# Forget logits of a gated attention layer computed beside the first head's projection instead of by matmuls of their own

## The chip, the cores and the metric

The kernel runs on one core of a Trainium2 chip. A core has a matmul engine (TensorE, "PE" in the profile, with its weight loads shown apart as "PEld"), a vector engine (DVE), a scalar engine (ACT), GpSimd (POOL), and queues that start DMAs (here almost all from SyncE, SP). The engines run side by side, each through its own list of instructions in order, and wait for each other through semaphores. The metric is the device time of one execution in microseconds (us). Positions in the trace are given in us from the start of the span.

## What is computed

Two residual layers over x of 512 tokens by 1024. Layer 0 is block attention with rotary; layer 1 is forgetting attention, cut here to what matters:

```python
hdn = rms_norm(x, norm_g[i])                       # (1, 512, 1024)
proj = hdn @ b_w_in[j]                             # 4 * 1024 + 8 columns
q, k, v, z = jnp.split(proj[..., :4 * WIDTH], 4, axis=-1)
f_logit = (proj[..., 4 * WIDTH:] + b_f_bias[j]).astype(jnp.float32)
log_f = jax.nn.log_sigmoid(f_logit).transpose(0, 2, 1)   # (1, 8 heads, 512)
c = jnp.cumsum(log_f, axis=-1)
sc = q @ k.T * scale + (c[..., :, None] - c[..., None, :])
x = x + (merge_heads(softmax(mask(sc)) @ v) * jax.nn.silu(z)) @ w_out[i]
```

So each of the 8 heads needs one forget logit for each token: 8 columns of the input projection beside the 4096 of q, k, v and z. Their log sigmoids are summed along the tokens.

## The kernel before

Everything stays in SBUF. Each fp32 operand of a matmul is held as two fp32r tensors, a rounded high part and the rest (`_hi`, `_lo`), and each product is made of three matmuls (`three`, L321: high by high, high by low, low by high). The profile gives these three lines as L325, L326 and L327.

A "job" is one set of weights of 1024 by 512: a head's q, k, v and z columns, or half of an output projection. It comes in 8 chunks (k = 0 to 7) of 128 rows. For each chunk SP starts a DMA into `w_raw` (a ring of 4), ACT rounds it into `w_hi` (L586), and POOL writes the rest into `w_lo` (L1061). There are two slots of `w_hi` and `w_lo`, so that the next head's weights are made ready while PE works with this head's. PE waits for the last low part (`wlo_set`) before it starts the projection of a head.

For each head PE projects q, k and v of the four token tiles t (`qkv`, L372: 24 matmuls of 384 columns each, with the hidden state as stationary operand), and z of all tokens at once (`zproj`, L392: 24 matmuls of 512 columns). After each tile ACT sums the squares of q and k and copies v (`read_qkv`), POOL makes the root (`rstd_qk`: an add, L1077, and a power, L1079), and DVE writes v's low part (L801) and the normed q and k (L811). `turn_qk` transposes them on PE (L408), ACT and DVE split the result (`split_qk`, L631 and L835), and `scores` makes the products. In layer 1 `scores` also adds the summed logs by a matmul with `crows` (L429), for which PE waits on `c_set`. `period` interleaves a head's attention with the projection of the next head, so that PE has matmuls while other engines do the softmax. The order on each engine is written out by hand in `first`, `period` and `last`; nothing else sets it.

The forget logits are made once, in `first(1)`, between the tiles 1 and 2 of the second layer's first head. `forget` (L476) runs 16 matmuls of 512 columns with `wf` as stationary operand, a tensor of 40 columns whose first 8 hold the high part of the 8 weight columns and whose last 8 the low part. The result is 40 rows by 512 tokens in bank 4. ACT copies the low rows (L697), DVE adds the two and the bias (L933) and makes the negative absolute value (L936), ACT runs Exp (L701) and Ln (L703), DVE makes the log sigmoid (L942) and its running sum (`cumulate`, a scan over 512 tokens on 8 partitions, L946). ACT rounds the sums into `crows` (L709), DVE writes their rest (`split_c`, L951) and sets `c_set`.

ACT loads a table of functions (ACT_TABLE_LOAD) before Ln and again before the next Exp.

## Time and profile before

| what | value |
|---|---|
| median of 3 runs | 568.36 us (568.06 to 568.9) |
| the profiled execution: its own time | 567.49 us |
| its span | 565.7 us, 9786 instructions |
| granted TensorE clock | 1.0 of full speed |
| PE busy | 558.7 us of the span, 3118 matmuls |
| DVE, ACT, POOL busy | 342.6, 249.7, 268.2 us |

The span is what lies between the first and the last instruction; the execution's own time is 1.79 us longer. Busy time of PE is modelled, since matmuls overlap: the distance from one matmul's start to the next one's tells what one costs in a row of them.

### The profile page before, as it was taken

What the parts mean: (1) busy time and instruction counts of PE and PEld (TensorE: products, weight loads), DVE (VectorE), ACT (ScalarE), POOL (GpSimd) and SP (SyncE); (2) the same over time, 40 slices, a digit from 0 to 9 for tenths busy, and PEclk for the clock granted to TensorE, in tenths of its full rate; (3) what the DMA queues carried; (4) which work ended last, traced back from release to release, by engine and by line L of the source; (5) the groups of instructions that cost most, each with busy time, mean ns of one, the idle gap of its engine ahead of it and who ended that gap; (6) DMA issues with size and microseconds to landing.
All of it is one profiled execution on the core that took longest, in us unless ns stands there. A gap on an engine that the chain in (4) does not pass through costs nothing.

```text
span 565.7 us, 9786 instructions
## 1 busy us (share of the span) xinstructions
PE 558.7 (99%) x3118; PEld 516.2 (91%) x3118; DVE 342.6 (61%) x824; ACT 249.7 (44%) x762; POOL 268.2 (47%) x320
## 2 busy tenths in 40 slices
PE   6999999999999999999999999999999999999998
PEld 4999999999999999888888999999999999998887
DVE  3788585859594949473553755656565646464621
ACT  5737272626263636152544635444444444442400
POOL 5857272727171818162656454545353536360700
PEclk9999999999999999999999999999999999999999
DMA  9823132313131313123423261415140615030221
GB/s 263 231 61 110 57 93 57 94 56 93 56 93 56 96 52 104 45 76 110 123 68 83 83 102 34 104 35 130 28 121 24 112 30 130 24 124 2 74 94 56
DMA packets 77068, 47.82 MB, mean 85 GB/s; under 512 B 3953, under 2 KB 71281, under 8 KB 77042
## 3 DMA queue, kind: packets, MB, share of 16 engines
q1 hardware_dynamic: 77040, 47.49, 31.5%
q8 instruction: 14, 0.23, 0.2%
q14 instruction: 12, 0.10, 0.1%
q10 hardware_dynamic: 2, 0.00, 0.0%
HBM read 45.39 MB, written 2.10 MB: 84 GB/s over the span
## 4 chain that ended last, share of the span: by engine, by line
PE 98%; DMA 1%; SPq 0%; DVE 0%; ACT 0%; issue 0%
PE banks L325 26%; PE banks L326 26%; PE banks L327 26%; PE banks L456 5%; PE banks L441 3%; PE banks L408 2%; PE banks L426 2%; PE banks L430 2%; PE banks L425 2%; PE banks L357 1%; DMA first_raw<-in_a_w_in_dram 1%; PE banks L429 1%; PE banks L482 0%; PE banks L483 0%; SPq L292 0%; DVE hT_lo L782 0%
## 5 line engine op out<-in xcount | busy, mean ns | idle before, releaser
L1061 POOL TENSOR_TENSOR w_lo<-w_raw,w_hi 128x512 fp32r<-128x512 f32 x147 | 188.3, 1311 | 63.0 <-ACT w_hi L586 63.0
L325 PE MATMUL banks<-w_hi,hT_hi 128*128 128x384 f32 x512 | 175.6, 343 | 1.0 <-DVE hT_lo L782 1.0
L327 PE MATMUL banks<-w_hi,hT_lo 128*128 128x384 f32 x512 | 171.6, 335 | 0.0
L326 PE MATMUL banks<-w_lo,hT_hi 128*128 128x384 f32 x512 | 171.6, 335 | 0.0
L1077 POOL TENSOR_TENSOR msq<-ssq,eps 128x2 f32<-128x2 f32 x64 | 14.3, 224 | 186.4 <-ACT junk L622 186.3
L325 PEld LDWEIGHTS banks<-w_hi,hT_hi 128*128 128x128 f32 x512 | 96.5, 188 | 1.9 <-POOL w_lo L1061 1.6
L326 PEld LDWEIGHTS banks<-w_lo,hT_hi 128*128 128x128 f32 x512 | 96.5, 189 | 0.1
L327 PEld LDWEIGHTS banks<-w_hi,hT_lo 128*128 128x128 f32 x512 | 96.3, 188 | 0.0
L586 ACT ACTIVATE w_hi<-w_raw 128x512 fp32r<-128x512 f32 x148 | 85.0, 646 | 20.2 <-DMA w_raw<-in_b_w_in_dram 14.4
L622 ACT ACTIVATE junk<-banks 128x128 bf16<-128x128 f32 x128 | 34.3, 274 | 115.8 <-PE banks L327 115.8
L906 DVE RECIPROCAL gz<-gz 128x128 f32<-128x128 f32 x64 | 58.1, 931 | 0.5
L835 DVE TENSOR_TENSOR qkT_lo<-banks,qkT_hi 128x512 fp32r<-128x512 f32 x32 | 20.6, 686 | 56.2 <-ACT qkT_hi L631 56.2
L801 DVE TENSOR_TENSOR v_lo<-banks,v_hi 128x128 fp32r<-128x128 f32 x64 | 18.2, 286 | 57.0 <-ACT v_hi L625 56.8
L325 PE MATMUL banks<-w_hi,yT_hi 128*128 128x512 f32 (+1 forms) x136 | 51.9, 382 | 0.0
L327 PE MATMUL banks<-w_hi,yT_lo 128*128 128x512 f32 (+1 forms) x136 | 51.3, 377 | 0.0
L326 PE MATMUL banks<-w_lo,yT_hi 128*128 128x512 f32 (+1 forms) x136 | 51.2, 377 | 0.0
L326 PE MATMUL banks<-hT_lo,w_hi 128*128 128x512 f32 x128 | 50.0, 391 | 0.0
L325 PE MATMUL banks<-hT_hi,w_hi 128*128 128x512 f32 x128 | 49.9, 390 | 0.0
L327 PE MATMUL banks<-hT_hi,w_lo 128*128 128x512 f32 x128 | 49.9, 390 | 0.0
L1079 POOL TENSOR_TENSOR rstd<-msq,power 128x2 f32<-128x2 f32 x64 | 44.3, 692 | 5.0
L641 ACT ACTIVATE probs<-banks,negmax 128x512 f32<-128x512 f32 (+1 forms) x64 | 33.3, 526 | 29.3 <-DVE negmax L856 28.9
L631 ACT ACTIVATE qkT_hi<-banks 128x512 fp32r<-128x512 f32 x32 | 17.4, 596 | 62.5 <-PE banks L408 62.5
(113 smaller groups left out, 883.9 us busy)
## 6 DMA issues: line engine op xcount, KB each, us to landing
w_raw<-in_b_w_in_dram SPq DMA_DIRECT2D x64, 256.0 KB, 3.7
w_raw<-in_a_w_in_dram SPq DMA_DIRECT2D x52, 256.0 KB, 3.0
w_raw<-in_w_out_dram SPq DMA_DIRECT2D x32, 256.0 KB, 2.9
first_raw<-in_a_w_in_dram SPq DMA_DIRECT2D x12, 256.0 KB, 5.6
out_dram<-xs SPq DMA_DIRECT2D x7, 256.0 KB, 2.1
xs<-in_x_dram SPq DMA_DIRECT2D x3, 512.0 KB, 5.8
xs<-in_x_dram SPq DMA_DIRECT2D x2, 256.0 KB, 3.2
gz<-in_norm_g_dram SPq DMA_DIRECT2D x1, 512.0 KB, 3.7
```

What stands on the lines that cost most here:

```text
L325: pe.matmul(dst, ah, bh, start=first and m == 0, stop=False)
L326: pe.matmul(dst, ah, bl, start=False, stop=False)
L327: mm = pe.matmul(dst, al, bh, start=False, stop=last and m == n - 1)
L456: mm = pe.matmul(banks[:, Y_BANK, j * P:SEQ], a[:, s, j, :], b[:, PT_COL[j]:PT_COL[j] + w], start=n == 0, stop=n == len(work) - 1)
L586: act.activation(w_hi[:, slot, k, :], raw, ACT.Copy).then_inc(whi_set, 1)
L622: sq = act.activation(junk[:, m, :], banks[:, qkv_bank(layer, h, t), m * P:(m + 1) * P], ACT.Square, scale=SCALE, accum_out=ssq[:, t % 2, ...
L641: act.activation(probs[:, P_COL[t]:P_COL[t] + w], banks[:, bank, col:col + w], ACT.Exp, bias=negmax[:, t:t + 1], accum_out=rowsum[:, t:t + ...
L801: dve.tensor_tensor(v_lo[:, s, t, :], banks[:, qkv_bank(layer, h, t), 2 * P:3 * P], f32(v_hi[:, s, t, :]), ALU.subtract).then_inc(vlo_set, 1)
L835: dve.tensor_tensor(qkT_lo[:, m, :], banks[:, QT_BANK + m, :], f32(qkT_hi[:, m, :]), ALU.subtract).then_inc(qkTlo_set, 1)
L906: dve.reciprocal(part, part).then_inc(ez1_set, 1)
L1061: pool.tensor_tensor(w_lo[:, slot, k, :], raw, f32(w_hi[:, slot, k, :]), ALU.subtract).then_inc(wlo_set, by)
L1079: pool.tensor_tensor(rstd[:, t % 2, :], msq[:, t % 2, :], power[:, :], ALU.pow).then_inc(rstd_set, 1)
```

## The change

Rows of `w_hi` and `w_lo` grow from 512 to 528 columns. The job's weights sit at columns 16 to 527, and columns 8 to 15 of slot 0 hold the 8 forget columns, written once in layer 0 from `wf_raw` by ACT and DVE. Nothing else is written there, so that they are still in place when slot 0 holds the second layer's first head. For this head alone the projection's matmuls take columns 8 to 399: 392 instead of 384. Each of the four tiles then has its 8 logits ahead of q, k and v in the same bank, and all reads of the bank are shifted by 8 columns (`qkv_cols`).

`forget` and its 16 matmuls are gone. DVE adds the bias to each tile's 128 by 8 logits (`read_forget`), and all four tiles' logits (128 by 32) go through the log sigmoid in one go in `rot`. PE turns the four 128 by 8 pieces into 8 rows by 512 tokens in bank 4 (`turn_forget`, between `zproj` and `turn_qk`), and the scan reads them from there. On ACT, Exp and Ln now stand behind the reading of tile 3 and ahead of the rounding of the last two weight chunks of the next head, and `exp_z` ahead of `crows`. The bias comes by a broadcasting DMA of 128 by 8, issued by SP between the layers ahead of the second layer's weights; the small DMA at the start and POOL's zeroing of `wf` (L1087) are gone.

```diff
+W_AT = 16
+F_AT = W_AT - HEADS
+WIDE = W_AT + CH
...
-        w_hi = sb("w_hi", [P, 2, KC, CH], F32R)
-        w_lo = sb("w_lo", [P, 2, KC, CH], F32R)
+        w_hi = sb("w_hi", [P, 2, KC, WIDE], F32R)
+        w_lo = sb("w_lo", [P, 2, KC, WIDE], F32R)
...
-        wf = sb("wf", [P, KC, LO_ROW + HEADS], F32R)
-        fbias = sb("fbias", [HEADS, 1])
...
+        def q_at(layer, h):
+            return HEADS if layer == 1 and isinstance(h, int) and h == 0 else 0
+        def qkv_cols(layer, h, t, first, n=1):
+            at = q_at(layer, h) + first * P
+            return banks[:, qkv_bank(layer, h, t), at:at + n * P]
...
-        f_lo, f_all = spare[0:HEADS, 0:SEQ], spare[0:HEADS, SEQ:2 * SEQ]
-        f_exp = rot[:, :, :, :].rearrange("p a b n -> p (a b n)")[0:HEADS, :]
+        f_all = spare[0:HEADS, SEQ:2 * SEQ]
+        f_log = rot[:, 0, 0, :].rearrange("p (f t h) -> p f t h", f=4, t=TILES)
         ones = cos_t[:, :, :, :].rearrange("p a b n -> p (a b n)")[0:HEADS, SEQ:2 * SEQ]
+        fbias = cos_t[:, 1, 0, 0:HEADS]
...
-                sp.dma_start(fbias[:, :], b_f_bias[0].rearrange("(h o) -> h o", o=1)).then_inc(small_in, 16)
...
+                    sp.dma_start(fbias, b_f_bias[0].partition_broadcast(P)).then_inc(qk_gain_in, 16)
...
-                    mm = three(banks[:, qkv_bank(layer, h, t), 0:3 * P],
+                    cols = slice(W_AT - q_at(layer, h), W_AT + 3 * P)
+                    mm = three(banks[:, qkv_bank(layer, h, t), 0:cols.stop - cols.start],
                                [((hT_hi[:, k, t * P:(t + 1) * P], hT_lo[:, k, t * P:(t + 1) * P]),
-                                 (w_hi[:, slot, k, 0:3 * P], w_lo[:, slot, k, 0:3 * P]))], k == 0, k == KC - 1)
+                                 (w_hi[:, slot, k, cols], w_lo[:, slot, k, cols]))], k == 0, k == KC - 1)
...
+                if q_at(layer, h):
+                    pe.wait_ge(wf_split, 2)
+                    wait(pe, f_step, t - 1)
...
-            def forget():
-                pe.wait_ge(wf_split, 2)
-                pe.wait_ge(hTlo_set, 2 * TILES * LAYERS)
-                pe.wait_ge(pTlo_set, 3 * HEADS)
-                for k in range(KC):
-                    pe.matmul(banks[0:LO_ROW + HEADS, FORGET_BANK, :], wf[:, k, :], hT_hi[:, k, :], start=k == 0, stop=False)
-                    mm = pe.matmul(banks[0:LO_ROW + HEADS, FORGET_BANK, :], wf[:, k, :], hT_lo[:, k, :],
-                                   start=False, stop=k == KC - 1)
+            def turn_forget():
+                pe.wait_ge(f_step, 7)
+                for t in range(TILES):
+                    mm = pe.transpose(banks[0:HEADS, FORGET_BANK, t * P:(t + 1) * P], f_log[:, 3, t, :], ident[:, :])
                 mm.then_inc(f_done, 1)
...
-                    qkv(layer, 0, 0, 1)
-                    forget()
-                    qkv(layer, 0, 0, 2)
-                    qkv(layer, 0, 0, 3)
+                    for t in range(1, TILES):
+                        qkv(layer, 0, 0, t)
                 zproj(layer, 0, 0)
+                if layer == 1:
+                    turn_forget()
                 turn_qk(layer, 0)
...
-                    act.wait_ge(small_in, 32)
-                    act.activation(wf[:, :, 0:HEADS], wf_raw[:, :, :], ACT.Copy).then_inc(wf_split, 1)
+                    act.wait_ge(small_in, 16)
+                    act.activation(w_hi[:, 0, :, F_AT:W_AT], wf_raw[:, :, :], ACT.Copy).then_inc(wf_split, 1)
...
-                    act.wait_ge(f_done, 1)
-                    act.activation(f_lo, banks[LO_ROW:LO_ROW + HEADS, FORGET_BANK, :], ACT.Copy).then_inc(f_act, 1)
                     read_qkv(layer, 0, 0, 2)
                     split_w(layer, 1, 1, (4, 5))
-                    act.wait_ge(f_step, 2)
-                    act.activation(f_exp, f_exp, ACT.Exp, scale=-1.0).then_inc(f_act, 1)
-                    act.wait_ge(f_act, 2)
-                    act.activation(f_exp, f_exp, ACT.Ln, bias=1.0).then_inc(f_act, 1)
                     read_qkv(layer, 0, 0, 3)
+                if layer == 1:
+                    act.wait_ge(f_step, 5)
+                    act.activation(f_log[:, 1], f_log[:, 1], ACT.Exp, scale=-1.0).then_inc(f_act, 1)
+                    act.wait_ge(f_step, 6)
+                    act.activation(f_log[:, 2], f_log[:, 1], ACT.Ln).then_inc(f_act, 1)
                 split_w(layer, 1, 1, (6, 7))
+                exp_z(layer, 0)
                 if layer == 1:
-                    act.wait_ge(f_step, 4)
+                    act.wait_ge(f_step, 8)
                     act.wait_ge(consts_set, 1)
                     act.activation(crows[0:HEADS, :], f_all, ACT.Copy).then_inc(chi_set, 1)
-                exp_z(layer, 0)
                 split_qk(layer, 0)
...
-            def forget_logits():
+            def read_forget(t):
+                dve.wait_ge(vhi_set, TILES * HEADS + t + 1)
+                dve.tensor_tensor(f_log[:, 0, t, :], banks[:, t % 2, 0:HEADS], fbias[:, :], ALU.add).then_inc(f_step, 1)
+            def log_sigmoid():
+                f, e, ln, lf = (f_log[:, n] for n in range(4))
+                dve.wait_ge(f_step, TILES)
+                dve.scalar_tensor_tensor(out=e, in0=f, scalar=-1.0, in1=f, op0=ALU.mult,
+                                         op1=ALU.max).then_inc(f_step, 1)
                 dve.wait_ge(f_act, 1)
-                dve.scalar_tensor_tensor(out=f_all, in0=banks[0:HEADS, FORGET_BANK, :], scalar=fbias[:, 0:1], in1=f_lo,
-                                         op0=ALU.add, op1=ALU.add).then_inc(f_step, 1)
-                dve.wait_ge(f_step, 1)
-                dve.scalar_tensor_tensor(out=f_exp, in0=f_all, scalar=-1.0, in1=f_all, op0=ALU.mult,
-                                         op1=ALU.max).then_inc(f_step, 1)
+                dve.tensor_scalar(e, e, 1.0, None, ALU.add).then_inc(f_step, 1)
+            def log_forget():
+                f, e, ln, lf = (f_log[:, n] for n in range(4))
+                dve.wait_ge(f_act, 2)
+                dve.scalar_tensor_tensor(out=lf, in0=f, scalar=0.0, in1=ln, op0=ALU.min,
+                                         op1=ALU.subtract).then_inc(f_step, 1)
             def cumulate():
-                dve.wait_ge(f_act, 3)
-                dve.scalar_tensor_tensor(out=f_lo, in0=f_all, scalar=0.0, in1=f_exp, op0=ALU.min,
-                                         op1=ALU.subtract).then_inc(f_step, 1)
-                dve.wait_ge(f_step, 3)
+                dve.wait_ge(f_done, 1)
                 dve.wait_ge(ones_set, 1)
-                dve.tensor_tensor_scan(f_all, ones, f_lo, 0.0, ALU.mult, ALU.subtract).then_inc(f_step, 1)
+                dve.tensor_tensor_scan(f_all, ones, banks[0:HEADS, FORGET_BANK, :], 0.0, ALU.mult,
+                                       ALU.subtract).then_inc(f_step, 1)
...
-                    dve.tensor_tensor(wf[:, :, LO_ROW:LO_ROW + HEADS], wf_raw[:, :, :], f32(wf[:, :, 0:HEADS]),
+                    dve.tensor_tensor(w_lo[:, 0, :, F_AT:W_AT], wf_raw[:, :, :], f32(w_hi[:, 0, :, F_AT:W_AT]),
                                       ALU.subtract).then_inc(wf_split, 1)
                 else:
-                    dve.wait_ge(qk_gain_in, 32)
+                    dve.wait_ge(qk_gain_in, 48)
                     dve.tensor_scalar(cos_t[:, 0, 0, :], cos_t[:, 0, 0, :], SCALE, None, ALU.mult).then_inc(tables_set, 1)
                     dve.wait_ge(tables_set, 3)
+                    read_forget(0)
                     split_v(layer, 0, 0, 0)
                     split_hidden(layer, TILES - 1)
                     norm_qk(layer, 0, 0)
-                    split_v(layer, 0, 0, 1)
-                    norm_qk(layer, 0, 1)
-                    forget_logits()
-                    split_v(layer, 0, 0, 2)
-                    norm_qk(layer, 0, 2)
-                    split_v(layer, 0, 0, 3)
-                    norm_qk(layer, 0, 3)
+                    for t in range(1, TILES):
+                        read_forget(t)
+                        if t == TILES - 1:
+                            log_sigmoid()
+                        split_v(layer, 0, 0, t)
+                        norm_qk(layer, 0, t)
+                    log_forget()
                     cumulate()
...
-            pool.memset(f32(wf[:, :, :]), 0.0)
...
```

PE, from the end of z's projection of the second layer's first head to the next head's first matmuls. In the other operands `ident` is the unit matrix and `rot` holds the logs. Before:

```order
L326 MATMUL banks<-hT_lo,w_hi 128x512
L327 MATMUL banks<-hT_hi,w_lo 128x512
L408 MATMUL banks<-ident,qkn 128x128 [waits y_gated,qkTlo_set,qkn_set]
L408 MATMUL banks<-ident,qkn 128x128 x7
L325 MATMUL banks<-w_hi,hT_hi 128x384 [waits wlo_set,qkn_set]
```

With the change:

```order
L338 MATMUL banks<-hT_lo,w_hi 128x512
L339 MATMUL banks<-hT_hi,w_lo 128x512
L497 MATMUL banks<-ident,rot 8x128 [waits f_step]
L497 MATMUL banks<-ident,rot 8x128 x3
L424 MATMUL banks<-ident,qkn 128x128 [waits y_gated,qkTlo_set,qkn_set]
L424 MATMUL banks<-ident,qkn 128x128 x7
L337 MATMUL banks<-w_hi,hT_hi 128x384 [waits wlo_set,qkn_set]
```

Four transposes, behind a wait for the logs (`f_step`), have come in ahead of the eight of q and k; the wait for the next head's low weight parts (`wlo_set`) follows them as before.

ACT, from the Exp of the logs to the split of the turned q and k, with the reading of tile 3 (`junk`, `v_hi`) in it. Before:

```order
L701 ACTIVATE rot<-rot 8x512 [waits f_step]
L703 ACT_TABLE_LOAD
L703 ACTIVATE rot<-rot 8x512 [waits f_act]
L622 ACTIVATE junk,ssq<-banks 128x128 [waits ssq_set,rstd_set,a_done]
L622 ACTIVATE junk,ssq<-banks 128x128
L625 ACTIVATE v_hi<-banks 128x128
L586 ACTIVATE w_hi<-w_raw 128x512 [waits raw_in2]
L586 ACTIVATE w_hi<-w_raw 128x512 [waits raw_in3]
L709 ACTIVATE crows<-sin_t 8x512 [waits consts_set,f_step]
L662 ACT_TABLE_LOAD [waits gate_set]
L662 ACTIVATE gz<-banks 128x512 [waits z_done]
```

With the change:

```order
L635 ACTIVATE junk,ssq<-banks 128x128 [waits ssq_set,rstd_set,a_done]
L635 ACTIVATE junk,ssq<-banks 128x128
L638 ACTIVATE v_hi<-banks 128x128
L714 ACTIVATE rot<-rot 128x32 [waits f_step]
L716 ACT_TABLE_LOAD
L716 ACTIVATE rot<-rot 128x32 [waits f_step]
L599 ACTIVATE w_hi<-w_raw 128x512 [waits raw_in2]
L599 ACTIVATE w_hi<-w_raw 128x512 [waits raw_in3]
L675 ACT_TABLE_LOAD [waits gate_set]
L675 ACTIVATE gz<-banks 128x512 [waits z_done]
L722 ACTIVATE crows<-sin_t 8x512 [waits consts_set,f_step]
```

The Exp, the table load and the Ln have moved from ahead of the reading of tile 3 to between it and the last two weight roundings, and the rounding of the sums (`crows`) has moved behind z's Exp.

DVE, from the normed q and k of tile 2 to the scan. Before:

```order
L801 TENSOR_TENSOR v_lo<-banks,v_hi 128x128 [waits vhi_set]
L811 SCALAR_TENSOR_TENSOR qkn<-banks,rstd,cos_t 128x128 [waits qkn_set,rstd_set]
L811 SCALAR_TENSOR_TENSOR qkn<-banks,rstd,cos_t 128x128
L942 SCALAR_TENSOR_TENSOR sin_t<-sin_t,rot 8x512 [waits f_act]
L946 SCALAR_TENSOR_TENSOR sin_t<-cos_t,sin_t 8x512 [waits ones_set,f_step]
```

With the change:

```order
L945 TENSOR_TENSOR rot<-banks,cos_t 128x8 [waits vhi_set]
L951 SCALAR_TENSOR_TENSOR rot<-rot 128x32 [waits f_step]
L954 TENSOR_SCALAR rot<-rot 128x32 [waits f_act]
L813 TENSOR_TENSOR v_lo<-banks,v_hi 128x128 [waits vhi_set]
L823 SCALAR_TENSOR_TENSOR qkn<-banks,rstd,cos_t 128x128 [waits qkn_set,rstd_set]
L823 SCALAR_TENSOR_TENSOR qkn<-banks,rstd,cos_t 128x128
L960 SCALAR_TENSOR_TENSOR rot<-rot 128x32 [waits f_act]
L967 SCALAR_TENSOR_TENSOR sin_t<-cos_t,banks 8x512 [waits ones_set,f_done]
```

Three small steps have come in ahead of tile 3's v and q, k, one of them behind a wait for ACT's Exp; the scan's second input is now the bank (`banks`), and it waits for PE's transposes (`f_done`).

## Rows read from the trace of the kernel before

**Rows 1.** The page: busy time by engine, and the chain that ended last.
```profile
PE 558.7 (99%) x3118; PEld 516.2 (91%) x3118; DVE 342.6 (61%) x824; ACT 249.7 (44%) x762; POOL 268.2 (47%) x320
...
PE 98%; DMA 1%; SPq 0%; DVE 0%; ACT 0%; issue 0%
```
**Rows 2.** Timeline of PE (start, us, what): first forget matmul, first of tile 2.
```profile
294.96 0.40 PE L482 MATMUL banks<-hT_hi,wf 128*40 128x512 f32 x1
...
298.68 0.33 PE L325 MATMUL banks<-w_hi,hT_hi 128*128 128x384 f32 x1
```
**Rows 3.** Timeline of PE, from tile 3's last matmul to the first scores.
```profile
306.84 0.33 PE L327 MATMUL banks<-w_hi,hT_lo 128*128 128x384 f32 x1
307.02 0.39 PE L325 MATMUL banks<-hT_hi,w_hi 128*128 128x512 f32 x1
...
312.50 1.04 PE L408 MATMUL banks<-ident,qkn 128*128 128x128 f32 x8
313.30 0.42 PE L325 MATMUL banks<-w_hi,hT_hi 128*128 128x384 f32 x1
...
317.54 0.39 PE L425 MATMUL banks<-qkT_hi 128*128 128x512 f32 x1
```
**Rows 4.** Timeline of ACT, from the table load to the rounding of the sums.
```profile
305.40 1.28 ACT L703 ACT_TABLE_LOAD   x1
306.70 0.63 ACT L703 ACTIVATE rot<-rot 8x512 f32<-8x512 f32 x1
307.24 0.26 ACT L622 ACTIVATE junk<-banks 128x128 bf16<-128x128 f32 x1
...
307.74 0.27 ACT L625 ACTIVATE v_hi<-banks 128x128 fp32r<-128x128 f32 x1
307.89 1.16 ACT L586 ACTIVATE w_hi<-w_raw 128x512 fp32r<-128x512 f32 x2
312.94 0.63 ACT L709 ACTIVATE crows<-sin_t 8x512 fp32r<-8x512 f32 x1 [3.89 <-DVE sin_t L946]
```
**Rows 5.** Groups by line and shape: busy us, mean ns of one.
```profile
L689 ACT ACTIVATE wf<-wf_raw 128x64 fp32r<-128x64 f32 x1 | 0.3, 258 | 0.0
...
L982 DVE TENSOR_TENSOR wf<-wf_raw,wf 128x64 fp32r<-128x64 f32 x1 | 0.2, 214 | 0.0
```
**Rows 6.** Timeline of POOL beside it: tile 3's root, the last two low parts.
```profile
307.92 0.20 POOL L1077 TENSOR_TENSOR msq<-ssq,eps 128x2 f32<-128x2 f32 x1 [0.69 <-ACT junk L622]
308.19 0.69 POOL L1079 TENSOR_TENSOR rstd<-msq,power 128x2 f32<-128x2 f32 x1
308.85 1.29 POOL L1061 TENSOR_TENSOR w_lo<-w_raw,w_hi 128x512 fp32r<-128x512 f32 x1
...
310.09 1.74 POOL L1061 TENSOR_TENSOR w_lo<-w_raw,w_hi 128x512 fp32r<-128x512 f32 x1
```
**Rows 7.** Timeline of DVE beside it, from the log sigmoid to q and k.
```profile
309.45 1.23 DVE L942 SCALAR_TENSOR_TENSOR sin_t<-sin_t,rot 8x512 f32<-8x512 f32 x1
310.71 2.19 DVE L946 TENSOR_TENSOR_SCAN sin_t<-cos_t,sin_t 8x512 f32<-8x512 f32 x1
...
313.61 0.68 DVE L951 TENSOR_TENSOR crows<-sin_t,crows 8x512 fp32r<-8x512 f32 x1 [0.52 <-ACT crows L709]
316.00 1.29 DVE L835 TENSOR_TENSOR qkT_lo<-banks,qkT_hi 128x512 fp32r<-128x512 f32 x2 [1.72 <-ACT qkT_hi L631]
```
**Rows 8.** Timeline of SP, POOL and PE where the second layer begins.
```profile
258.00 0.43 SPq L311 DMA_DIRECT2D cos_t<-in_b_q_norm_dram  x1
258.48 0.43 SPq L312 DMA_DIRECT2D cos_t<-in_b_k_norm_dram  x1
...
281.72 3.02 POOL L1061 TENSOR_TENSOR w_lo<-w_raw,w_hi 128x512 fp32r<-128x512 f32 x2 [0.67 <-ACT w_hi L586]
...
285.32 0.42 PE L325 MATMUL banks<-w_hi,hT_hi 128*128 128x384 f32 x1
```

29 lines of the change are left out of this document (15 added, 14 removed).

## The prediction, made before the changed kernel was run

> **What bounds the kernel.** I read the page first. PE is busy in 99% of the span and makes 98% of the chain that ended last [rows 1], so the time is the sum of what PE issues plus the few moments in which it waits. A microsecond taken from PE's list counts in full, if nothing that PE waits for comes due in its place. What other engines gain or lose counts only there. Next comes PE's timeline at the place of the change, for the distance from one start to the next [rows 2, 3]. Last come the timelines of ACT, POOL and DVE beside it, for how much earlier than PE they finish [rows 4, 6, 7].
>
> **What PE loses.** The 16 forget matmuls start at 294.96 and the first matmul of tile 2 follows at 298.68 [rows 2]: 3.72 us, nothing hidden.
>
> **What PE gets: wider projections.** 96 matmuls take 8 more columns. From 298.68 to 307.02 lie 48 matmuls of 384 columns [rows 2, 3], 0.1738 us each; from 307.02 to 312.50 lie 24 of 512 [rows 3], 0.2283 each. The difference is 0.0546 us for 128 columns, so 8 columns cost 0.0034 and 96 such matmuls 0.33 us. No row shows a width of 392 or a weight row of 528 columns. From below the eight columns cost 0 (a price by blocks of columns), from above what a 512-column matmul costs, 96 x 0.0546 = 5.2 us. I take 0.33, since the two widths shown lie on one line with a small constant (0.1738 - 384 x 0.00043 = 0.01 us).
>
> **What PE gets: four transposes.** Eight transposes take 313.30 - 312.50 = 0.80 us [rows 3], 0.10 each. The new ones move 128 columns too, with 8 columns of weights instead of 128. From above 0.40 us, from below what 128 columns alone cost at the rate above, 4 x 0.055 = 0.22. I take 0.40, the same operation at the same place.
>
> **The sum without waits** is -3.72 + 0.33 + 0.40 = -2.99 us.
>
> **New waits.** I count from P, the end of the first head's q, k, v projection (307.02 in rows 3). With the change PE reaches the end of z's projection at P+5.48 as before, ends the four transposes at P+5.88 and the eight at P+6.68, and then needs the next head's last low weight part; the scores come 4.24 us later (317.54 - 313.30), at P+10.92. Three things must be there.
>
> (a) The logs, for the four transposes, at P+5.48. Tile 3's last matmul ends at 307.17, ACT's reading starts at P+0.22, and v_hi ends at 308.01, P+0.99 [rows 3, 4]. DVE adds the bias (about 0.2, as the 64-element step took 0.214 [rows 5]) and starts on the negative absolute value at P+1.22, ending about P+1.4. ACT's Exp takes about 0.25 (64 elements took 0.258 [rows 5]), to P+1.7. The table load takes 1.28 and Ln follows it at once (305.40 + 1.28 = 306.68, Ln at 306.70 [rows 4]); DVE's addition of one hides behind the load. Ln ends at about P+3.2 and the log sigmoid at P+3.5: 2 us early, no cost.
>
> (b) The low weight parts of the next head, at P+6.68. This chain got longer, since Exp, load and Ln now stand ahead of the last two roundings. ACT starts on chunk 6 at about P+3.1 and ends it at P+3.75 (two take 1.16 [rows 4]); POOL's two parts take 1.29 and about 1.25 [rows 6], to P+6.35. Before it was 311.83, P+4.81, against a need at P+6.28: 1.47 us of slack fall to 0.3. Even that rests on DVE's step at P+1.22 starting freely. POOL's power for tile 3 ran from 308.19 for 0.69, P+1.17 to P+1.86 [rows 6]. Now look at the other pair: DVE's log sigmoid with both inputs in SBUF began at 309.45, while POOL worked until 310.14, and took 1.23, and the same size with POOL idle took 0.68 [rows 6, 7]. It ran, then, from 310.00 to 310.68, and POOL's next part took 1.74 instead of 1.29. One waits for the other to end. If the power holds DVE's step (both inputs in SBUF) likewise, the whole chain moves by about 0.55 us, to P+6.9, and PE waits 0.2 us and then loads its first weights without cover, 0.1 more: 0.3 us. If DVE's step comes first, 0. I take 0.3, as the power's start is 0.05 us ahead by these rows. The Trainium skill ("SBUF — State Buffer", "SBUF: two separate sides") calls this an exclusive lock, held for a whole instruction, when DVE has two SBUF inputs; by that rule the step waits too, and the trace agrees with the rule in the pair above.
>
> (c) The sums (`c_set`) and the turned q and k, at P+10.92. From the end of z's projection, Z = P+5.48: the transposes end at Z+0.64 (eight took 1.04, the next start was 0.24 before that), DVE scans from Z+0.69. If the scan takes 2.19 as before, `crows` runs from Z+2.92 to Z+3.55, its rest to Z+4.27, and q and k (1.29 [rows 7], the first overlapping) to Z+5.48, P+10.96: 0.04 us late, with PE's weights uncovered 0.1 to 0.2 us. But the old scan began at 310.71, while POOL's part ran until 311.83, and both its inputs were in SBUF; by the reading above its own work was about 1.1 us. The new one reads the bank, so I take 1.1 and no cost, with 1.0 us of slack. This end too reaches from 0 to 0.2.
>
> **What is hidden.** DVE's four small additions lie where DVE is idle; they delay v and q, k of their tile by 0.2 us, and PE needs these two tiles later. The bias DMA makes SP's queue about 0.47 us longer (258.00 to 258.48 for the like [rows 8]) ahead of the second layer's weights. PE needs their last low part at 285.32; it was done at 284.74 [rows 8], and that was set by ACT's order behind PE's transposes, not by the load. Cost 0; uncovered it would be 0.47. POOL's zeroing and the early DMA lie beside PE's start, which waits for the input: 0.
>
> **The sum.** -2.99 + 0.3 = -2.7 us against the execution's own 567.49: 564.8. The median of the runs is 0.87 higher, so I forecast 568.36 - 2.7 = 565.7.
>
> **Rivals.**
> - The low weight parts come much later: ACT's chain is on PE's path, and every us in it costs one. Were a switch of tables to cost a second load time (another 1.28), they would be ready at P+7.6 to 8.2, PE would wait 1.0 to 1.6, and the time would be 566.4 to 567.0. Against it: Ln followed the load by 0.02 us [rows 4]. The Trainium skill ("ScalarE: Activation LUTs", "What ACT_TABLE_LOAD costs") gives a switch 2.66 us with a drain, which is this rival; the row speaks against it.
> - No new wait at all, and transposes near their lower end: -3.72 + 0.33 + 0.22 = -3.17, 565.2.
> - Slower than before: a 392-column matmul is billed as a 512-column one, at 96 places, because it is no whole number of 128-column pieces or crosses the pieces of a row. Price 5.2 instead of 0.33: +2.2 us, 570.6. It decides from 0.03 us extra a matmul on. Nothing in the trace has such a width, so I can't exclude it; that q, k and v are one piece of 384 in the same bank speaks against it.
> - The change takes PE's work away and the time is given back, since a transfer or another engine sets the pace of the second layer: 567.4 to 568.9. Against it: PE is idle in 1% of the span, and other engines are at most 61% busy [rows 1].
>
> **How the numbers follow.** Forecast, with 0 to 0.5 us of waits (565.3 to 566.0): 0.62. No wait and cheap transposes (565.0 to 565.3): 0.15. Late weights (566.0 to 567.2): 0.14. Given back: 0.05. Slower: 0.04. The range leaves out the last two and little more of the others: 564.9 to 566.9. A measurement of this kernel can tell about 0.2%, 1.1 us. Faster by more than that (below 567.2): 0.91; within: 0.05; slower: 0.04.
>
> **What would show it.** In the profile of the changed kernel: no 40-column matmuls; 392-column matmuls 0.177 us apart; four transposes in 0.2 to 0.4 us; the log chain with its load between tile 3's v and chunk 6; the low part of chunk 7 ending within 0.4 us of PE's need; a scan of about 1.1 us. Wrong would be a wait of PE over 0.5 us at the next head's first projection or at its scores, or another distance of the wide matmuls.

## The result: slower, by 3.9 us

| | median of the runs, us | lowest to highest | profiled execution | its span |
|---|---|---|---|---|
| before | 568.63 (4 runs) | 568.06 to 569.48 | 567.49 | 565.7 |
| changed | 572.52 (4 runs) | 571.67 to 572.62 | 571.67 | 569.9 |

The ratio is 1.0067, with a 95% interval of 1.0051 to 1.0083. The forecast was 565.7, faster. The time lies 6.8 us above it and outside the range.

The page of the changed kernel, busy time by engine and the chain that ended last, answers to [rows 1]:

```profile
PE 562.6 (99%) x3106; PEld 518.9 (91%) x3106; DVE 340.7 (60%) x828; ACT 248.2 (44%) x761; POOL 268.0 (47%) x319
...
PE 95%; DMA 2%; DVE 1%; SPq 1%; ACT 0%; POOL 0%; issue 0%; DVEq 0%
```

PE has 12 matmuls less (16 out, 4 in) and yet 3.9 us more of busy time. It is 99% busy as before, so the time went into its matmuls, not into waiting. The next question is which matmuls. At the place of the change the distances are nearly as before. Here is PE's timeline (start, us, what) from tile 3's last matmul to the first scores, which answers to [rows 3]:

```profile
307.44 0.34 PE L339 MATMUL banks<-w_hi,hT_lo 128*128 128x392 f32 x1
307.62 0.40 PE L337 MATMUL banks<-hT_hi,w_hi 128*128 128x512 f32 x1
...
313.18 0.60 PE L497 MATMUL banks<-ident,rot 128*8 128x128 f32 x4
313.62 1.04 PE L424 MATMUL banks<-ident,qkn 128*128 128x128 f32 x8
314.41 0.42 PE L337 MATMUL banks<-w_hi,hT_hi 128*128 128x384 f32 x1
...
318.72 0.40 PE L441 MATMUL banks<-qkT_hi 128*128 128x512 f32 x1
```

The 24 matmuls of z take 313.18 - 307.62 = 5.56 us, where [rows 3] have 5.48, and the 24 of the next tile 4.31 instead of 4.24. That is about 1.5% too much, and the first layer, where the change adds no work at all, is slower as well. These are the starts of z's projection of two neighbouring heads of the first layer, in the kernel before:

```profile
199.69 0.39 PE L325 MATMUL banks<-hT_hi,w_hi 128*128 128x512 f32 x1
...
227.65 0.39 PE L325 MATMUL banks<-hT_hi,w_hi 128*128 128x512 f32 x1
```

and in the changed kernel:

```profile
202.17 0.39 PE L337 MATMUL banks<-hT_hi,w_hi 128*128 128x512 f32 x1
...
230.42 0.39 PE L337 MATMUL banks<-hT_hi,w_hi 128*128 128x512 f32 x1
```

One head takes 28.25 us instead of 27.96. The busy times on the page don't show this well, because the ends of matmuls are modelled; the distance from start to start does. Its means over the whole trace, in ns, worked out from the starts of PE's timeline (distances with a wait in them are left out):

| matmul (the profile names the moving operand first) | before | changed |
|---|---|---|
| 384 columns, moving w_hi, fixed hT_hi | 174.0 | 175.3 |
| 384, moving w_lo, fixed hT_hi | 173.8 | 177.5 |
| 384, moving w_hi, fixed hT_lo | 173.9 | 174.5 |
| 512, z: moving hT_hi, fixed w_hi | 227.8 | 230.3 |
| 512, z: moving hT_hi, fixed w_lo | 227.8 | 230.3 |
| 512, z: moving hT_lo, fixed w_hi | 228.4 | 234.9 |
| 512, output projection: w_hi with yT_hi, w_lo with yT_hi, w_hi with yT_lo | 227.2, 227.2, 227.3 | 230.2, 233.5, 231.6 |

Per three products that is 5.6 ns (384 columns), 11.5 (z) and 13.6 (output), and 480 x 5.6 + 128 x 11.5 + 120 x 13.6 ns = 2.7 + 1.5 + 1.6 = 5.8 us. (The output projection has 16 more sets of three with half the columns, which got no slower.)

All these matmuls read `w_hi` or `w_lo`, but they are not the only ones that changed. The 384 matmuls of the attention itself (`qkT`, `pT`, `v`), which read neither, take 60.67 us by the same distances instead of 60.12, 0.55 more. Some of them got slower and some faster. The last one ahead of the first z above is an example. It takes 224 ns before:

```profile
199.46 0.39 PE L456 MATMUL banks<-pT_hi,v_lo 128*128 128x512 f32 x1
```

and 236 ns in the changed kernel, up to z's start at 202.17:

```profile
201.93 0.40 PE L472 MATMUL banks<-pT_hi,v_lo 128*128 128x512 f32 x1
```

What differs for the matmuls with weights is the address. By the sizes in their declarations `hT_hi`, `hT_lo`, `w_hi`, `w_lo` and `yT_hi` begin 16384, 24576, 32768 and 32768 bytes one behind the other in each partition of the kernel before. All these are multiples of 256, and their rows of 512 columns are 2048 bytes apart. So all rows stand at the same place modulo 256. With 528 columns the weight rows are 2112 bytes apart and their data begin 64 bytes later, so that they stand at four different places modulo 256 in turn. The arrays of the attention have moved too, but by 2048 bytes, a multiple of 256.

### The profile page after: what moved, and what is told of

Read it like the earlier page. It is cut to its first block, busy times and chain, and to the rows that moved or that the text cites. A ratio compares the mean times of both kernels' runs of the same rounds, so it can differ in the third digit from the quotient of the medians.

```text
span 569.9 us, 9766 instructions
## 1 busy us (share of the span) xinstructions
PE 562.6 (99%) x3106; PEld 518.9 (91%) x3106; DVE 340.7 (60%) x828; ACT 248.2 (44%) x761; POOL 268.0 (47%) x319
## 4 chain that ended last, share of the span: by engine, by line
PE 95%; DMA 2%; DVE 1%; SPq 1%; ACT 0%; POOL 0%; issue 0%; DVEq 0%
PE banks L337 26%; PE banks L338 25%; PE banks L339 25%; PE banks L472 5%; PE banks L457 3%; PE banks L424 2%; PE banks L446 2%; PE banks L442 2%; PE banks L441 2%; PE banks L369 1%; DMA w_raw<-in_b_w_in_dram 1%; DMA first_raw<-in_a_w_in_dram 1%; PE banks L445 1%; DVE qkn L782 0%; POOL w_lo L1084 0%
## 5 line engine op out<-in xcount | busy, mean ns | idle before, releaser
L337 PE MATMUL banks<-w_hi,hT_hi 128*128 128x384 f32 (+1 forms) x512 | 177.2, 346 | 1.2 <-DVE hT_lo L794 1.2
L338 PE MATMUL banks<-w_lo,hT_hi 128*128 128x384 f32 (+1 forms) x512 | 174.0, 340 | 0.0
L339 PE MATMUL banks<-w_hi,hT_lo 128*128 128x384 f32 (+1 forms) x512 | 172.8, 338 | 0.0
```

The lines of the kernel that those rows point to most:

```text
L337: pe.matmul(dst, ah, bh, start=first and m == 0, stop=False)
L338: pe.matmul(dst, ah, bl, start=False, stop=False)
L339: mm = pe.matmul(dst, al, bh, start=False, stop=last and m == n - 1)
```

## The experiments

Theory A: the layout of the weight rows, and not the eight extra columns or a new wait, makes the time; without it the change gives what the forecast's sum says. Rival: the time is lost in the second layer, in work or waits that the change adds.

**1. The rows alone.** The kernel before, with the weight rows widened and nothing else of the change:

```
+W_AT = 16
+WIDE = W_AT + CH
-        w_hi = sb("w_hi", [P, 2, KC, CH], F32R)
-        w_lo = sb("w_lo", [P, 2, KC, CH], F32R)
+        w_hi = sb("w_hi", [P, 2, KC, WIDE], F32R)
+        w_lo = sb("w_lo", [P, 2, KC, WIDE], F32R)
...
-                             (w_hi[:, 1, k, w], w_lo[:, 1, k, w])) for k in range(HEADS)], True, True)
+                             (w_hi[:, 1, k, wa], w_lo[:, 1, k, wa])) for k in range(HEADS)], True, True)
```

> The kernel before with only the rows of w_hi and w_lo made 528 columns long (the weights at columns 16 to 527, columns 0 to 15 unused), at the same addresses as in the changed kernel. The forget matmuls and all else stay; to make room wf lies in crows, which POOL zeroes again after them. Theory A (where the rows lie slows the matmuls that read them): the distance of the 384-column matmuls rises from 0.174 to about 0.176 to 0.177 us and that of the 512-column ones from 0.227 to about 0.231, in sum 6 to 7 us: 574.5 to 575.5. Theory B (the loss comes from the steps that the change adds, their waits or the 392-column matmuls): no change, 568.6.

Measured: 574.73 us against 568.48, ratio 1.0105 (1.0083 to 1.0128). The layout alone costs 6.25 us, close to the 5.8 and 0.55 summed above. Each kind of matmul with weights has the distance of the changed kernel within 0.3 ns, and the attention's take 60.66 us, as there. One head of the first layer takes 28.26 us, as in the changed kernel:

```profile
203.13 0.39 PE L326 MATMUL banks<-hT_hi,w_hi 128*128 128x512 f32 x1
...
231.39 0.39 PE L326 MATMUL banks<-hT_hi,w_hi 128*128 128x512 f32 x1
```

**2. The change without the rows.** The changed kernel with rows of 512 columns. There is no room for forget columns in them, so it reads z's first eight columns in their place; the forget logits are those of other weights:

```
-W_AT = 16
-F_AT = W_AT - HEADS
-WIDE = W_AT + CH
+W_AT = 0
+WIDE = CH
...
-                    cols = slice(W_AT - q_at(layer, h), W_AT + 3 * P)
+                    cols = slice(0, 3 * P + q_at(layer, h))
```

> The changed kernel with rows of 512 columns as before. The second layer's first head takes the first eight columns of z in place of the forget columns (392 neighbouring columns, the same matmuls, reads, transposes and scan), so the logits are not the reference's. Theory A: the whole loss goes and the forecast's sum is left, -2.7 to -3.0 against before: 565.6 to 565.9. Theory B: it stays at 572.5.

Measured: 566.27 us, ratio 0.9958 (0.9945 to 0.9972), 2.2 us faster than before and a little above what theory A expected. The two effects add up: 2.2 less and 6.25 more would make 4.0 more, and 3.9 was measured. But the sum without waits said -3.0, so 0.8 us is missing; experiments 5 to 7 go after it.

**3. Another distance, in one slot.** The changed kernel with slot 1's rows 2048 bytes apart and slot 0's 2176 (544 columns, data 128 bytes from the start of a row):

```
-W_AT = 16
+W_AT = 32
...
+            def make(self, slot):
+                setattr(self, f"t{slot}", sb(f"{self.name}{slot}", [P, KC, self.wide if slot == 0 else CH], F32R))
```

> The changed kernel, the computation whole, with slot 1 of w_hi and w_lo in rows of 512 columns as before (it holds no forget columns) and slot 0 in rows of 544 (2176 bytes, weights from byte 128 of a row), so that every row and every start is a whole multiple of 128 bytes. If theory A holds and a multiple of 128 bytes is what counts, nothing is left of the loss: 565.6 to 566.0. If theory A holds but the rows must lie a multiple of 256 bytes or more apart, half of the matmuls (those of slot 0) are still slow: 568.5 to 569.5. Theory B: 572.5.

Measured: 568.84 us, ratio 1.0004 (0.9994 to 1.0014). It is 2.6 us slower than rows_of_512, so a distance that is a multiple of 128 bytes still costs. Only half of the matmuls read slot 0. There three products take 6.6 ns (384 columns) and 10.4 ns (z) more than in slot 0 of the kernel before, about as much as with 528 columns in the changed kernel (6.7 and 11.1); in slot 1 they are back within 0.2 ns. The attention's matmuls take 60.11 us, as before, although their arrays lie where they lie in the changed kernel. So what slows these is not their own address.

**4. The sweep.** A kernel of its own that computes nothing of the reference and was run once: 32 matmuls for each layout in one accumulation, eight rows of the moving and eight of the fixed operand in turn, with starts and distances varied.

```
+            def go(bank, n, last, moving_at, moving_row, fixed_at, fixed_row, width):
+                k = n % 8
+                a = (moving_at + moving_row * k) // 4
+                b = (fixed_at + fixed_row * k) // 4
+                return banks[:, bank, 0:width], fixed[:, b:b + P], moving[:, a:a + width], n == 0, n == last - 1
```

> No part of the layers: it copies x to the output and runs 44 stretches of 32 fp32r matmuls (the first one of 160) on rounded pieces of x, one after the other with nothing beside them. Each stretch has its own start and row distance of the moving and of the stationary operand. Theory A: stretches whose rows start at multiples of 2048 bytes run at 0.1735 us a matmul of 384 columns and 0.227 of 512, and some of those with starts or row distances off that raster (64 bytes, rows of 2112) 2 to 9 ns slower. Theory B: all stretches of one width are alike within 1 ns.

Some rows of PE's timeline of it, one for each layout, all with 384 columns. L96 has the fixed operand 128 bytes further on, L99 256; L129, L132 and L135 have the moving operand's rows 2176, 2304 and 2560 bytes apart; L138 is the base:

```profile
121.77 5.79 PE L96 MATMUL banks<-moving,fixed 128*128 128x384 f32 x32
127.40 5.71 PE L99 MATMUL banks<-moving,fixed 128*128 128x384 f32 x32
...
183.08 5.76 PE L129 MATMUL banks<-moving,fixed 128*128 128x384 f32 x32
188.68 5.71 PE L132 MATMUL banks<-moving,fixed 128*128 128x384 f32 x32
194.23 5.71 PE L135 MATMUL banks<-moving,fixed 128*128 128x384 f32 x32
199.78 5.71 PE L138 MATMUL banks<-moving,fixed 128*128 128x384 f32 x32
```

From L96's start to L99's are 127.40 - 121.77 = 5.63 us, from L129's to L132's 5.60, but from L132's to L135's and from L135's to L138's 5.55. The means within each stretch, without its first four, are clearer (ns):

| layout | 384 columns | 512 columns |
|---|---|---|
| base: both rows 2048 bytes apart, same place modulo 256 | 173.3 | 227.6 |
| moving operand 16 / 32 / 64 / 128 / 192 bytes further | 175.6 / 173.3 / 173.3 / 176.2 / 176.6 | not run / 233.3 / 228.9 / 232.4 / not run |
| moving operand 256 / 512 / 1024 further | 173.7 / 173.3 / 173.3 | |
| fixed operand 16 / 32 / 64 / 128 further | 173.3 / 173.4 / 174.7 / 175.9 | not run / not run / 233.3 / not run |
| fixed operand 256 / 512 / 1024 further | 173.3 | |
| both 32 / 64 / 128 / 256 further | 173.7 / 173.7 / 173.7 / 173.3 | |
| moving rows 2080 / 2112 / 2176 bytes apart | 175.9 / 175.2 / 175.0 | not run / 232.0 / 230.1 |
| moving rows 2304 / 2560 apart | 173.3 / 173.3 | |
| fixed rows 2112 / 2176 apart | 174.1 / 176.7 | 231.7 / 232.5 |
| fixed rows 2304 / 2560 apart | 173.3 / 173.3 | |
| 392 columns, base / 32 bytes further and rows 2112 apart | 177.2 / 179.3 | |

Every start and distance that keeps the two operands and all their rows at the same place modulo 256 bytes runs within 0.4 ns of the base. Where they disagree most layouts cost 0.8 to 3.4 ns at 384 columns and 1.3 to 5.7 at 512. Disagreement isn't always dear, as the shifts at 384 columns show that are free. The moving operand's rows 2112 bytes apart take 175.2 ns (384 columns) and 232.0 (512) here, the fixed one's 231.7 (512). In the changed kernel the means of the three products are 175.8, 231.8 (output) and 231.8 (z).

The sweep says less than it seems, since within a stretch all matmuls are of one kind. Where kinds follow one another the distances differ even in agreement: in the kernel before, z's first three matmuls behind the attention's take 231, 236 and 228 ns, later ones 226 and 227. So a neighbour counts too, which fits what the attention's matmuls did above. No run takes the neighbours apart: whether the moving operand meets the fixed operand of its own matmul or that of the next one, whose load overlaps it, is open.

**5. The changed kernel in a layout that agrees.** Slot 0's rows are 576 columns, 2304 bytes or nine times 256, with the data 256 bytes from the start of a row. The memory for it comes from the area reserved for DMA descriptors, 16384 bytes, which this kernel can do with 12288 of. It has a second repair, the bias's transfer at the start of the kernel, which experiment 6 tries by itself:

```
-W_AT = 32
+W_AT = 64
...
-    nc = bacc.Bacc("TRN2", target_bir_lowering=False, num_devices=1)
+    nc = bacc.Bacc("TRN2", target_bir_lowering=False, num_devices=1, dynamic_dma_scratch_size=12288)
```

> The whole changed kernel, complete, with two repairs: slot 0's weight rows lie 576 columns (2304 bytes, nine times 256) apart with the data 256 bytes from the row's start, slot 1's 512 columns apart, room made by 4096 bytes less of the area reserved for DMA descriptors; and the bias goes to a buffer of its own at the start of the kernel instead of at the layer boundary. Theory (distances and offsets that are multiples of 256 bytes cost nothing; the bias transfer costs about 1 us at the boundary): 384-column matmuls 173.9 ns apart in both slots, 512-column ones 227.7; time 565.2 to 565.8. Rival 1 (any row other than 2048 bytes costs, whatever its multiple): slot 0's matmuls 175 to 177 ns, 230 and more; 567.5 to 569. Rival 2 (the bias transfer has no part in the lost microsecond): 566.2 to 566.8.

Measured: **565.17 us** against 568.28, ratio 0.9940 (0.9927 to 0.9954). This is the whole kernel, and it beats both. Its 384-column matmuls are 173.8 to 173.9 ns apart, z's 227.7 to 228.3, the output's 227.0 to 227.5. In these runs the width of a row does no harm; its remainder modulo 256 does. The first layer's head is back at 27.96 us:

```profile
200.31 0.39 PE L356 MATMUL banks<-hT_hi,w_hi 128*128 128x512 f32 x1
...
228.27 0.39 PE L356 MATMUL banks<-hT_hi,w_hi 128*128 128x512 f32 x1
```

**6. The bias transfer.** PE's timeline of rows_of_512 has a wait at the layer boundary, where hidden tile 0 of the second layer is turned:

```profile
272.14 0.60 PE L369 MATMUL banks<-ident,qkn 128*128 128x128 f32 x4
273.54 0.66 PE L369 MATMUL banks<-ident,qkn 128*128 128x128 f32 x4 [0.81 <-DVE qkn L782]
273.95 0.47 PE L337 MATMUL banks<-w_hi,yT_hi 128*128 128x512 f32 x1
```

In the kernel before the eight run in one piece:

```profile
271.65 1.03 PE L357 MATMUL banks<-ident,qkn 128*128 128x128 f32 x8
272.44 0.48 PE L325 MATMUL banks<-w_hi,yT_hi 128*128 128x512 f32 x1
```

The place is held for 1.81 us instead of 0.79. The kernel with rows of 512 columns was run again beside one in which the bias is loaded at the start into a buffer of its own:

```
+        fbias = sb("fbias", [P, HEADS])
...
-        fbias = cos_t[:, 1, 0, 0:HEADS]
...
+                sp.dma_start(fbias[:, :], b_f_bias[0].partition_broadcast(P)).then_inc(small_in, 16)
...
-                    sp.dma_start(fbias, b_f_bias[0].partition_broadcast(P)).then_inc(qk_gain_in, 16)
```

> The kernel with weight rows of 512 columns (forget logits from z's first eight columns in place of the forget columns), with the bias loaded into a buffer of its own at the start of the kernel, so that nothing new stands in SP's queue ahead of the second layer's weights. Theory (the bias transfer delays the first low weight part of the second layer by about 1 us, and PE's turns of the hidden state wait): no wait of PE at the turn of the hidden state of tile 0, 1 us less than the same kernel with the transfer at the boundary, 565.1 to 565.6. Rival (the lost microsecond comes from elsewhere, such as POOL's low parts and DVE's normalization getting in each other's way): same time, 566.0 to 566.6.

> The same kernel as rows_of_512, as the partner of bias_at_the_start on the same chip: 566.3, with PE's wait at the turn of tile 0 of the hidden state (0.8 us) at the layer boundary.

Measured: 565.26 us with the early bias, 566.16 with the bias at the boundary (568.28 before), ratios 0.9941 (0.9927 to 0.9954) and 0.9962 (0.9948 to 0.9975). The wait is gone in the first and is there again in the second:

```profile
274.64 0.66 PE L369 MATMUL banks<-ident,qkn 128*128 128x128 f32 x4 [0.58 <-DVE qkn L782]
```

The intervals of the ratios just overlap, but all five times with the early bias (up to 565.50) lie below all five of its partner (from 565.88), the traces part the two at this place, and the next run shows the transfer by itself.

**7. The transfer in the kernel before.**

```
                     sp.dma_start(cos_t[:, 0, 1, :], b_k_norm[0].partition_broadcast(P)).then_inc(qk_gain_in, 16)
+                    sp.dma_start(cos_t[:, 1, 0, 0:HEADS], b_f_bias[0].partition_broadcast(P)).then_inc(qk_gain_in, 16)
...
-                    dve.wait_ge(qk_gain_in, 32)
+                    dve.wait_ge(qk_gain_in, 48)
```

> The kernel before with nothing but a third broadcast transfer (the forget bias, 32 bytes for each of 128 partitions, into an unused corner of cos_t) ahead of the second layer's weights in SP's queue. Theory: it alone costs 0.7 to 1.0 us, 569.3, and PE waits at the turn of the hidden state of tile 0. Rival: no cost, 568.4 to 568.7.

Measured: 569.62 us against 568.28, ratio 1.0019 (1.0010 to 1.0028). A transfer of 4 KB costs 1.3 us by the medians, 1.1 by the ratio and 0.96 at its place in the trace: some 1 us. Its way to PE can be followed. The starts of this run are 0.40 us later than in the kernel before all through the first layer, which has to be taken off. SP issues the transfer, POOL's first low part of the new weights comes next, then DVE's normalization of tile 0, then PE:

```profile
259.34 0.43 SPq L313 DMA_DIRECT2D cos_t<-in_b_f_bias_dram  x1
...
266.27 1.28 POOL L1062 TENSOR_TENSOR w_lo<-w_raw,w_hi 128x512 fp32r<-128x512 f32 x1 [10.62 <-ACT w_hi L587]
...
270.90 2.44 DVE L771 SCALAR_TENSOR_TENSOR qkn<-xs,ssx,gz 128x512 f32<-128x512 f32 x2 [3.41 <-POOL ssx L1071]
...
272.05 0.60 PE L358 MATMUL banks<-ident,qkn 128*128 128x128 f32 x4
273.39 0.66 PE L358 MATMUL banks<-ident,qkn 128*128 128x128 f32 x4 [0.75 <-DVE qkn L771]
273.80 0.48 PE L326 MATMUL banks<-w_hi,yT_hi 128*128 128x512 f32 x1
```

In the kernel before the same two steps are

```profile
264.93 1.29 POOL L1061 TENSOR_TENSOR w_lo<-w_raw,w_hi 128x512 fp32r<-128x512 f32 x1 [9.68 <-ACT w_hi L586]
...
269.48 1.41 DVE L770 SCALAR_TENSOR_TENSOR qkn<-xs,ssx,gz 128x512 f32<-128x512 f32 x2 [2.39 <-POOL ssx L1070]
```

The low part is late by 266.27 - 264.93 - 0.40 = 0.94 us, twice the 0.47 that SP needs to issue. ACT's rounding ahead of it waits for the weights and is late by as much (265.56 against 264.23, less the 0.40), while SP starts the weights' DMAs only 0.46 later (260.14 against 259.28, less the same). Why they land later still isn't shown. The normalization, which waits for POOL's root behind that part, starts 1.02 late and takes 1.03 longer, because another low part of POOL (from 271.22, for 1.57) holds the second of its two steps; experiment 8 shows such a hold by itself. So it ends at 273.34, 2.05 us later than before, at 270.89. PE needs its second half at 272.05 + 0.4; a cover of about 1.2 us is used up, and PE loses 1.75 - 0.79 = 0.96.

**8. DVE and POOL in pairs.** The prediction had DVE's |f| step wait for POOL's power, and it did not. A kernel that computes nothing of the reference measured one DVE step at a time alone, beside POOL's subtraction and beside its power.

```
+                if beside == "sub":
+                    pool.tensor_tensor(low[:, :], xs[:, 2, 0:SEQ], xs[:, 3, 0:SEQ], ALU.subtract).then_inc(pool_done, 1)
+                elif beside == "pow":
+                    pool.tensor_tensor(root[:, :], pos[:, 0:2], half[:, :], ALU.pow).then_inc(pool_done, 1)
```

> A kernel of its own that computes nothing of the reference: one DVE step at a time, three times each, alone (after POOL has ended), beside POOL's 128x512 subtraction from SBUF (sub), and beside POOL's power of 128x2 (pow). DVE's steps, each behind a 128x128 lead step so that POOL has started: the negative absolute value of 128x32 (f32) and of 128x512 (f512) with both inputs in SBUF, the scan of 8x512 with both inputs in SBUF (scan) and with one in a bank (scanb). Reading of the prediction (a DVE step with two SBUF inputs waits for POOL's instruction to end, whichever it is): f32, f512 and scan take longer beside both, by up to 0.5 us beside the power and 1.0 beside the subtraction; scanb as alone, 1.2. Rival (only the subtraction, which moves many elements, holds it; the power spends its 0.69 us elsewhere): nothing is longer beside the power, f32 stays at 0.19; beside the subtraction as above. Second rival (nothing waits for an end, the two share the port step by step): beside the subtraction f32 stays near 0.2 and f512 and the scan get longer by a share.

The groups of this kernel by line and shape (count, busy us, mean ns of one); the tile's name says what ran beside it:

```profile
L71 POOL TENSOR_TENSOR low<-xs 128x512 f32<-128x512 f32 x12 | 15.6, 1301 | 10.4 <-ACT tick L64 10.4
L73 POOL TENSOR_TENSOR root<-pos,half 128x2 f32<-128x2 f32 x12 | 8.8, 730 | 7.1 <-ACT tick L64 7.1
...
L90 DVE TENSOR_TENSOR_SCAN scan_sub<-xs 8x512 f32<-8x512 f32 x3 | 6.8, 2275 | 0.0
L86 DVE SCALAR_TENSOR_TENSOR f_sub<-xs 128x512 f32<-128x512 f32 x3 | 5.2, 1750 | 0.0
L86 DVE SCALAR_TENSOR_TENSOR f_sub<-xs 128x32 f32<-128x32 f32 x3 | 3.8, 1251 | 0.0
L90 DVE TENSOR_TENSOR_SCAN scan_alone<-xs 8x512 f32<-8x512 f32 x3 | 3.6, 1205 | 0.0
...
L90 DVE TENSOR_TENSOR_SCAN scanb_sub<-xs,banks 8x512 f32<-8x512 f32 x3 | 3.6, 1201 | 0.0
...
L86 DVE SCALAR_TENSOR_TENSOR f_alone<-xs 128x32 f32<-128x32 f32 x3 | 0.6, 186 | 0.0
L86 DVE SCALAR_TENSOR_TENSOR f_pow<-xs 128x32 f32<-128x32 f32 x3 | 0.6, 185 | 0.0
```

Beside the subtraction each DVE step with both inputs in SBUF is longer by the same 1.07 us, whatever its own length (1.25 for 0.19, 1.75 for 0.69, 2.28 for 1.21): it waits nearly to POOL's end, and then runs. It goes on 0.13 us ahead of the end that the profile gives for POOL (a step from 27.90 to 29.15 beside a subtraction from 27.80 to 29.10, for example). The second rival falls. The scan with one input in a bank isn't held at all. Beside the power, which takes POOL 0.73 us, nothing is held, though DVE's steps start 0.10 behind it as they do behind the subtraction. The first rival stands: it depends on POOL's instruction. Whether the power's two elements or its operation makes the difference stays open. The old scan in [rows 7], with both inputs in SBUF, fits: 2.19 us are 0.98 of hold and its own 1.21, and the hold ends 0.14 ahead of the end of POOL's part at 311.83.

**9. The offset without the distance.** The kernel before, its weight arrays 64 bytes further on and their rows still 2048 apart:

```
+        ahead = sb("ahead", [P, 16])
         w_hi = sb("w_hi", [P, 2, KC, CH], F32R)
         w_lo = sb("w_lo", [P, 2, KC, CH], F32R)
+        behind = sb("behind", [P, 48])
```

> The kernel before, with both weight arrays moved on by 64 bytes and their rows left 2048 bytes apart (64 bytes of filler ahead of them and 192 behind, so that all later arrays move by 256). It parts the offset from the distance of the rows. Theory (what counts is where the moving and the fixed operand lie against each other modulo 256 bytes, as in the sweep, whose stretches with one of the two moved by 64 bytes differ from its base by 0 (384, moving), +1.3 ns (512, moving) and +5.7 ns (512, fixed)): q, k, v matmuls stay at 173.9 ns, z's go from 228 to some 233, the output projection's from 227.3 to some 228.6; 384 x 5.7 ns + 400 x 1.3 ns = +2.7 us, 570.5 to 571.5. Rival 1 (only the distance from row to row counts): 568.2 to 568.7, all distances as before. Rival 2 (any disagreement costs alike, as with rows of 528 columns): +5 to +6.5 us, 574.

Measured: 569.70 us against 568.42, ratio 1.0021 (1.0012 to 1.0031). The matmuls behave much as in the sweep: 384 columns at 173.1 to 173.8 ns, no dearer than before; z's at 232.6 to 233.4 instead of 227.8 to 228.4. The output's are at 228.1 to 230.6 instead of 227.2 to 227.3, one of the three well above the 1.3 ns of the sweep. Both rivals fall: the distance alone doesn't decide, and not every disagreement costs. The sum was put too high, +2.7 where +1.3 was measured. The means give 384 x 4.9 ns = 1.9 for z and 360 x 1.9 ns = 0.7 for the output, less 0.3 for its 48 matmuls of half the columns (113 ns instead of 120) and 0.6 for q, k and v, which came out up to 0.9 ns cheaper, hence 1.7. From the first z on, where its start-up is left behind, the trace is 1.7 us longer than the one before. The remaining 0.4 us to the median isn't explained.

## Why the prediction was wrong, point by point

**The step that failed: the price of the matmuls.** "No row shows a width of 392 or a weight row of 528 columns" stood in the text, but only the width got a price, at 96 places. The row of 528 columns touches every matmul that reads weights, some 2,300 of them, and was taken at 0 there without a sentence. It cost 5.8 us at these matmuls and 0.55 at the attention's by the distances, and 6.25 in all by experiment 1. The rival that ended slower had the wrong mechanism and the wrong place: it billed the 96 wide matmuls as 512 columns, 228 ns, and these came at 175.8 to 181.2 ns. A hint stood in [rows 2]: the 16 forget matmuls take 3.72 us, 232.5 ns each, where other 512-column matmuls take 228.3 in [rows 3], and their weight rows are 160 bytes apart. The prediction used that number and didn't ask why it was larger.

**What PE loses and gets: right.** From the first z on to P the kernel of experiment 5 is 304.25 - 32.60 = 271.65 us, the kernel before 307.02 - 31.98 = 275.04: -3.39, the forecast's -3.72 + 0.33. That it fits to the hundredth is luck, since the wide matmuls alone came 0.1 us dearer. The four transposes take 313.62 - 313.18 = 0.44 us in the changed kernel, forecast 0.40. The 392-column matmuls are 178.0 ns apart in the mean in the changed kernel and 178.3 in that of experiment 5, forecast 177.2, some 0.1 us in all. So one sign of being wrong that the prediction named, another distance of the wide matmuls, showed next to nothing; the loss lay in the matmuls that the change doesn't widen. -2.99 was the right sum for a change in a good layout: experiment 5 measured -3.1 in the medians.

**(a) The logs: right.** ACT's timeline of the changed kernel, which answers to [rows 4], with P at 307.62:

```profile
308.33 0.28 ACT L638 ACTIVATE v_hi<-banks 128x128 fp32r<-128x128 f32 x1
309.07 0.23 ACT L714 ACTIVATE rot<-rot 128x32 f32<-128x32 f32 x1 [0.46 <-DVE rot L951]
309.32 1.28 ACT L716 ACT_TABLE_LOAD   x1
310.61 0.23 ACT L716 ACTIVATE rot<-rot 128x32 f32<-128x32 f32 x1
310.75 1.14 ACT L599 ACTIVATE w_hi<-w_raw 128x512 fp32r<-128x512 f32 x2
```

v_hi ends at P+0.99 and Ln at P+3.22, as forecast (P+0.99, P+3.2). The table load takes 1.28 us and Ln follows 0.01 behind it, so the rival of a doubled switch falls.

**(b) The low parts: the time right, the 0.3 us wrong.** DVE's timeline at the place, answering to [rows 7], (c) with it:

```profile
308.84 0.19 DVE L951 SCALAR_TENSOR_TENSOR rot<-rot 128x32 f32<-128x32 f32 x1
...
313.81 1.21 DVE L967 TENSOR_TENSOR_SCAN sin_t<-cos_t,banks 8x512 f32<-8x512 f32 x1 [2.75 <-PE banks L497]
...
316.44 1.29 DVE L847 TENSOR_TENSOR qkT_lo<-banks,qkT_hi 128x512 fp32r<-128x512 f32 x2
```

and POOL's, answering to [rows 6]:

```profile
308.79 0.69 POOL L1102 TENSOR_TENSOR rstd<-msq,power 128x2 f32<-128x2 f32 x1
311.44 2.55 POOL L1084 TENSOR_TENSOR w_lo<-w_raw,w_hi 128x512 fp32r<-128x512 f32 x2 [1.96 <-ACT w_hi L599]
```

The |f| step starts 0.05 us behind POOL's power, the very order that the forecast took, and ends 0.19 later, while the power runs for 0.69. So the parts end at P+6.37, against a forecast of P+6.35 without the hold, and PE comes at P+6.79 and doesn't wait. The step carried a reading of one pair (a subtraction) over to another instruction (the power). Experiment 8 shows that the first holds DVE and the second doesn't. The rule of the Trainium skill ("SBUF — State Buffer", "SBUF: two separate sides"), by which a DVE instruction with two SBUF inputs and a GpSimd instruction that reads SBUF lock each other out for a whole instruction, fits the subtraction, 1.07 us, and not the power, 0.00 us, though that reads SBUF as well. This step of the forecast was wrong by its 0.3 us and had no part in the loss.

**(c) The scan: right.** 1.21 us, forecast 1.1. In the changed kernel POOL's part ends 0.18 us after the scan's start, so this trace hardly tries the reason given; experiment 8 does, and an input in a bank isn't held. q and k end at 317.73, 0.99 us ahead of the scores at 318.72; forecast 1.0.

**The hidden bias transfer: wrong.** It was put at 0, "uncovered it would be 0.47". It cost 0.9 us with rows of 512 columns. In the changed kernel PE's turn holds 276.37 - 275.12 = 1.25 us instead of 0.79, so 0.46:

```profile
275.12 0.60 PE L369 MATMUL banks<-ident,qkn 128*128 128x128 f32 x4
275.95 0.66 PE L369 MATMUL banks<-ident,qkn 128*128 128x128 f32 x4 [0.23 <-DVE qkn L782]
276.37 0.48 PE L337 MATMUL banks<-w_hi,yT_hi 128*128 128x512 f32 x1
```

Two things failed. The need was looked up at PE's first use of the last low part, at 285.32 in [rows 8]; what came due first was another product of the same queue, POOL's root for tile 0, which PE needs 13 us earlier. And the price was SP's issue alone, while the first weights came later by 0.94.

**The sum again.** -2.99, + 0.1 for the 392-column matmuls, + 0.46 for the transfer, + 6.25 for the layout make +3.8 us. Measured +3.9.

## What to carry to other kernels

A change of an array's shape is a change for every instruction that reads it; count those first, and price the new address pattern as well as the new work. For fp32r matmuls like these keep rows and starts of both operands at the same place modulo 256 bytes, which was never dearer here, and where a few extra columns are needed, pad the row to the next multiple of 256 even if memory has to be found for it. A "hidden" transfer is hidden only if every product behind it in the queue has room, the small ones too that stand behind a large one on a slow engine.
